# The last down piece of a mixture of experts cut into column halves, gate rows made in the third pair, identity products kept for the first layer only

## What is computed

```
hid = silu(einsum('nd,edf->enf', n, w_gate)) * einsum('nd,edf->enf', n, w_up)
hid = hid * gates.T[:, :, None]
moe = einsum('enf,efd->nd', hid, w_down)
xp = xp + gf_p * moe(prompt rows)
xs = xs + gf_s * moe(sample rows)
```

## Time and profile before

| | |
|---|---|
| median of 3 runs | 1241.68 us (1240.28 to 1242.07) |
| the profiled execution's own time | 1242.56 us |
| its span from first to last instruction | 1240.7 us |
| PE busy | 94% of the span |
| DVE, ACT, POOL busy | 23%, 15%, 5% |
| chain that ended last | PE 74%, DMA 20%, issue 2%, DVE 1% |
| read from HBM | 490.72 MB |

### The profile page before, as it was taken

One profiled execution on the slowest core, in us unless ns is written; L12 is line 12 of the kernel. 1 busy time (PEld: TensorE's weight loads), 2 busy tenths in 40 slices (PEclk: granted clock), 3 DMA queues, 4 the chain that ended last, 5 costly groups with the idle time before them and its releaser, 6 DMA issues.

```text
span 1240.7 us, 13760 instructions
## 1 busy us (share of the span) xinstructions
PE 1170.5 (94%) x5531; PEld 514.7 (41%) x5531; DVE 279.6 (23%) x673; ACT 187.5 (15%) x441; POOL 56.4 (5%) x68
## 2 busy tenths in 40 slices
PE   4999999999998889899999999999999898898998
PEld 2445465443433333334334454743434324343432
DVE  1146533121020101021232354312021010202013
ACT  1225322000000000001022333210000100000010
POOL 0412000000000000000013100000000000000000
PEclk9999999999999999999999999999999999999999
DMA  9999999999999999999998559899999999999996
GB/s 375 389 387 369 415 424 429 423 430 428 429 424 429 430 426 429 430 427 427 421 389 268 196 214 398 359 376 407 426 426 428 427 428 428 429 428 427 430 422 282
DMA packets 60948, 494.18 MB, mean 398 GB/s; under 512 B 5586, under 2 KB 6754, under 8 KB 30052
## 3 DMA queue, kind: packets, MB, share of 16 engines
q1 hardware_dynamic: 57856, 485.88, 94.7%
q0 software_dynamic: 2864, 7.46, 1.8%
q10 hardware_dynamic: 180, 0.17, 0.0%
HBM read 490.72 MB, written 3.16 MB: 398 GB/s over the span
## 4 chain that ended last, share of the span: by engine, by line
PE 74%; DMA 20%; issue 2%; SPq 2%; DVE 1%; ACT 1%; POOL 0%; DVEq 0%; ACTq 0%
PE bank L1195 40%; PE bank L944 9%; DMA ring<-in_w_up 8%; DMA ring<-in_w_gate 5%; DMA ring<-in_w_down 3%; PE bank L1223 3%; PE bank L954 3%; PE bank L1145 3%; DMA ring<-in_w_mod 3%; PE bank L899 3%; PE bank L1156 3%; PE bank L877 2%; PE bank L961 1%; PE bank L1256 1%; PE bank L999 1%
## 5 line engine op out<-in xcount | busy, mean ns | idle before, releaser
L1195 PE MATMUL bank<-ring,hT 128*64 128x512 f32 x2520 | 576.5, 608 | 43.9 <-issue 20.3
L1195 PEld LDWEIGHTS bank<-ring,hT 128*64 128x64 f32 x2520 | 191.0, 140 | 399.8 <-issue 392.2
L944 PE MATMUL bank<-ring,hT 128*128 128x512 f32 x320 | 140.2, 595 | 2.7 <-DMA ring<-in_w_in_ab 2.4
L944 PEld LDWEIGHTS bank<-ring,hT 128*128 128x128 f32 x320 | 59.8, 190 | 78.5 <-issue 75.7
L2014 DVE TENSOR_TENSOR work<-work,bank 128x512 f32<-128x512 f32 x56 | 38.5, 688 | 163.4 <-PE bank L1156 163.2
L2007 DVE TENSOR_TENSOR work<-work,bank 128x512 f32<-128x512 f32 x32 | 22.0, 687 | 221.3 <-PE bank L1195 197.8
L1195 PE MATMUL bank<-work,hT 128*64 128x512 f32 x284 | 69.4, 593 | 0.0
L1145 PE MATMUL bank<-work 128*128 128x128 f32 x512 | 61.4, 278 | 0.3 <-DVE rc L2056 0.3
L1145 PEld LDWEIGHTS bank<-work 128*128 128x128 f32 x512 | 59.8, 195 | 2.0 <-issue 1.6
L1533 ACT ACTIVATE hT<-bank 128x512 f32<-128x512 f32 x32 | 19.0, 595 | 257.3 <-PE bank L1256 257.3
L2066 DVE COPY work<-bank 128x512 f32<-128x512 f32 x14 | 9.7, 692 | 205.5 <-PE bank L1195 205.5
(11 more groups left out here) (223 smaller groups left out, 756.9 us busy)
## 6 DMA issues: line engine op xcount, KB each, us to landing
ring<-in_w_gate SPq DMA_DIRECT2D x56, 2048.0 KB, 17.8
ring<-in_w_up SPq DMA_DIRECT2D x50, 2048.0 KB, 17.2
ring<-in_w_down SPq DMA_DIRECT2D x46, 2048.0 KB, 16.9
ring<-in_w_mod SPq DMA_DIRECT2D x23, 2048.0 KB, 10.9
work<-in_w_up SPq DMA_DIRECT2D x8, 2048.0 KB, 15.2
ring<-in_w_down SPq DMA_DIRECT2D x12, 1024.0 KB, 14.3
ring<-in_w_in_c SPq DMA_DIRECT2D x6, 2048.0 KB, 21.7
ring<-in_w_in_ab SPq DMA_DIRECT2D x4, 2048.0 KB, 21.3
```

The source lines that it names most:

```text
L944: ins = pe.matmul(b[:, 0:n], hT[:, c, t * P:(t + 1) * P], w[:, c, 0:n], start=i == 0, stop=i == DC - 1)
L1195: ins = pe.matmul(bank[banks[j]][64 * e:64 * e + 64, :], lhs[:, 4 * h + c, 64 * e:64 * e + 64], weights(e, c, j), start=(h, c) == (0, 0), ...
```

## The change

Four edits:

- The last piece, row chunk 3 of units 10 and 11, is loaded and multiplied in two: its left 512 columns, then its right 512. `LAST_PIECES` gets a fourth entry, the range of `j`. PE does the scatter of (1, 0) between the two.
- DVE gates in the order (1, 0), (0, 0), (1, 1), (0, 1), so both products of the left bank come first. PE scatters in layer 1 in that order, in layer 0 in the order (1, 0), (1, 1), (0, 0), (0, 1).
- The four matmuls that spread the gate rows, and ACT's four copies, stand in pair 2 in place of the last pair.
- The identity products of t = 1 are made in layer 0 only. In layer 1 all four quarters of `x` are ended by an addition on DVE, and the result is written out in the gating order.

```
-LAST_PIECES = [(6, 0, 2), (6, 2, 4), (8, 0, 2), (8, 2, 4), (10, 0, 2), (10, 2, 3), (10, 3, 4)]
+LAST_PIECES = [(6, 0, 2, range(2)), (6, 2, 4, range(2)), (8, 0, 2, range(2)), (8, 2, 4, range(2)),
+               (10, 0, 2, range(2)), (10, 2, 3, range(2)), (10, 3, 4, range(1)), (10, 3, 4, range(1, 2))]
+GATED_ORDER = [(1, 0), (0, 0), (1, 1), (0, 1)]
+SCATTER_ORDER = {0: [(1, 0), (1, 1), (0, 0), (0, 1)], 1: GATED_ORDER}
...
@@ last_units, SP
-                            cols = slice(D * c0, D * c1)
-                            sp.dma_start(flat[slot][:, cols], src[:, cols]).then_inc(last_ld[l][i], 16)
+                            cols = slice(D * c0 + UC * js[0], D * (c1 - 1) + UC * (js[-1] + 1))
+                            sp.dma_start(flat[slot][:, cols], src[:, cols]).then_inc(last_ld[i], 16)
...
@@ last_product, PE
-                        pe.wait_ge(last_ld[l][i], 32)
-                        for j in range(2):
+                        pe.wait_ge(last_ld[i], 32 * (l + 1))
+                        for j in js:
...
+                        if (k, c1, js[-1]) == (10, 4, 0):
+                            scatter_gated(0)
...
-                def last_scatter():
-
-                    for t in (1, 0):
-                        for h in range(2):
-                            pe.wait_ge(m["yd_gated"], 3 - 2 * t + h)
-                            pe.matmul(last_bank(t, h)[:, :], GT[:, t, :], ydg[t][:, h * UC:(h + 1) * UC],
-                                      start=t == 0, stop=True).then_inc(m["scattered"], 1)
+                def scatter_gated(i):
+
+                    t, h = SCATTER_ORDER[l][i]
+                    pe.wait_ge(m["yd_gated"], 1 + GATED_ORDER.index((t, h)))
+                    pe.matmul(last_bank(t, h)[:, :], GT[:, t, :], ydg[t][:, h * UC:(h + 1) * UC],
+                              start=(l, t) != (0, 1), stop=True).then_inc(m["scattered"], 1)
...
@@ pair, PE
                     if final:
                         scatter(n)
                         gates_transposed(n)
-                        pe.wait_ge(m["y_added"], 4 * n + 4)
-                        expert_gate_rows(1)
-                        expert_gate_rows(0)
                     product(n, 0, (0, 1), hgT, m["hg_ready"])
...
                     product(n, 2, (0, 1), hgT, m["hg_ready"], m["gate_half"])
+                    if isinstance(n, int) and n == 2:
+                        pe.wait_ge(m["y_added"], 4 * n + 4)
+                        expert_gate_rows(1)
+                        expert_gate_rows(0)
...
-                        last_product(n, 8, (6, 7), hidT, None, 0)
+                        last_product(n, 8, (6, 7), hidT, None, None if l else 0)
                         pe.wait_ge(m["ht_ready"], 2 * n + 2)
-                        row_first(n, 1)
+                        if l == 0:
+                            row_first(n, 1)
...
@@ pair, DVE
                     if final:
                         gate_down(1, 0)
+                        gate_down(0, 0)
                         dve.wait_ge(moe_used[l], used(n, 11))
                         gate_down(1, 1)
+                        gate_down(0, 1)
                         return
...
@@ end of layer 1, DVE
-                    gate_down(0, 0)
-                    gate_down(0, 1)
-                    for u in range(2):
-                        row_out(end, u)
-                    for u in range(2):
-                        add_last(end, 0, u)
+                    for t, u in SCATTER_ORDER[1]:
+                        add_last(end, t, u)
```

More of the change, by code:

```diff
@@ L393, in build @@
         moe_ld = [[sem(f"moe_loaded{l}_{i}") for i in range(SLOTS)] for l in range(LAYERS)]
-        last_ld = [[sem(f"last_loaded{l}_{i}") for i in range(len(LAST_PIECES))] for l in range(LAYERS)]
+        last_ld = [sem(f"last_loaded{i}") for i in range(len(LAST_PIECES))]
         ahead_ld = [[sem(f"ahead_loaded{l}_{e}") for e in range(2)] for l in range(LAYERS)]
@@ L634, in last_units @@
                         load_in_turn(k, at[k % 2], n * MOE_UNITS + (k + 1))
-                    for i, (k, c0, c1) in enumerate(LAST_PIECES):
+                    for i, (k, c0, c1, js) in enumerate(LAST_PIECES):
                         w, order = (a["w_up"], "(p h r) -> h p r") if k < 8 else (a["w_down"], "(h p r) -> h p r")
@@ L758, in _ @@
             experts(1)
-            for t, name in ((1, "y_sample"), (0, "y_prompt")):
-                for u in range(2):
-                    cols = slice(u * UC, (u + 1) * UC)
-                    sp.wait_ge(x_ready, 4 * 3 + 2 * (1 - t) + u + 1)
-                    sp.dma_start(a[name][:, cols], x[:, t, cols]).then_inc(out_y, 16)
+            for i, (t, u) in enumerate(SCATTER_ORDER[1]):
+                cols = slice(u * UC, (u + 1) * UC)
+                sp.wait_ge(x_ready, 4 * 3 + i + 1)
+                sp.dma_start(a[("y_prompt", "y_sample")[t]][:, cols], x[:, t, cols]).then_inc(out_y, 16)
             sp.wait_ge(out_y, 64)
@@ L1213, in last_product @@
                     slots = [moe_slot(l, k + e - OUTSIDE) for e in range(2)]
-                    for i, (unit, c0, c1) in enumerate(LAST_PIECES):
+                    for i, (unit, c0, c1, js) in enumerate(LAST_PIECES):
                         if unit != k:
@@ L1295, in pair @@
                         last_product(n, 6, (2, 3), hgT, m["up_half"])
-                        pe.wait_ge(m["gates_ready"], 4)
                     else:
@@ L1300, in pair @@
                         pe.wait_ge(m["y_added"], 4 * n + 4)
+                    if isinstance(n, int) and n == 2:
+                        pe.wait_ge(m["gates_ready"], 4)
                     hidden_transposed(n, 0)
@@ L1328, in experts @@
                 pair(more * PAIRS + (PAIRS - 1), final=True)
-                last_scatter()
+                for i in range(1, 4):
+                    scatter_gated(i)
             pe.wait_ge(ld_first, 16)
@@ L1547, in pair @@
                                    ACT.Copy).then_inc(m["gt_ready"], 1)
-                    if final:
+                    sigmoid(n, 0)
+                    sigmoid(n, 1)
+                    if isinstance(n, int) and n == 2:
                         for i, (t, u) in enumerate(((1, 0), (1, 1), (0, 0), (0, 1))):
@@ L1551, in pair @@
                             act.activation(gbuf[:, 2 * t + u, :], bank[4 + 2 * t + u][:, :], ACT.Copy).then_inc(m["gates_ready"], 1)
-                    sigmoid(n, 0)
-                    sigmoid(n, 1)
                     hidden_transposed(n, 0)
@@ L2039, in add_last @@
                 def add_last(n, t, u):
-                    count, cols = 2 * (1 - t) + u + 1, slice(u * UC, (u + 1) * UC)
+                    count, cols = 1 + SCATTER_ORDER[l].index((t, u)), slice(u * UC, (u + 1) * UC)
                     dve.wait_ge(m["scattered"], 4 * n + count)
```

## The result

| | before | after |
|---|---|---|
| median | 1241.70 us (1240.02 to 1244.80, 8 runs) | 1246.61 us (1244.66 to 1250.48, 8 runs) |
| the profiled execution's time and span | 1242.56, 1240.7 | 1244.66, 1242.9 |

The ratio of after to before is 1.0038, with a 95% interval of 1.0027 to 1.0049: 4.7 us slower. The predicted time was 1246.2 us.

A forecast was written before the change was run, and what follows sets the result against it. The weight stream sets the pace in both mixtures of experts, PE running neck and neck with it in the last pairs. Layer 0's 1.4 + 1.9 and layer 1's 1.3 - 0.1 give +4.5 on 1241.68: 1246.2 us, range 1242.8 to 1248.5.

The forecast's parts named there:

- a lead of 0.3: Last pair, units 4 and 5: PE, ready earlier, starts their product 0.3 us sooner, still held by unit 5's landing.
- the early scatter: Scatter between the last piece's halves delays bank 7's gating: 1.9 us at layer 0's hand-over, 1.3 at layer 1's end.
- Rival D: Layer 0's hand-over: its 1.9 us is partly hidden by other waiting; +1.2 us in all, 1242.9, chance 0.15.
- T: Start of the unit-10 product in a layer's last pair; 1226.59 in layer 1 before the change.
- Rival C: Layer 0's hand-over: the clock falls once more at PE's stops, 1.7 us more; +6.2, 1247.9, chance 0.1.
- The new wait and the early arrival of PE: Last pairs: without the gate rows PE is ready sooner, then waits some 2.7 us for units 4 and 5.
- Rival E: Last pair: PE is the bound and the stream lands early enough to follow; -7.6 us, 1234.1, chance 0.09.
- rival B: Layer 0's last pair: the clock does not fall behind the new wait; +3.0 us in all, 1244.7, chance 0.2.
- So I take a fall here, in both layers: Clock falls behind the wait for units 4 and 5, costing 1.7 us; layer 0's unit-10 product starts 1.4 late.
- The identity products in layer 1: Two products of 1.1 us each leave layer 1's last pair; their 2.2 us absorb the slow clock, unit 10 0.1 early.
- I cost the move at nothing: Gate rows' 3.7 us in pair 2 of each layer cost nothing, covered by PE's waits and the loads' spare time.
- the stream's reserve: Pair 2: the load with least in hand has some 7.6 us of its 17.46 to spare, more than the rows' 3.7.

The follow-up runs named there:

- after_again: The changed kernel, unaltered, run once more: 1246.99 us, ratio 1.0038 against the kernel before.
- rows_back: The changed kernel with the gate rows and their copies back at the head of the last pair: 1244.68 us, ratio 1.0025 against the kernel before.
- rows_at_wait: The changed kernel with the gate rows in the last pair, between its gate and up products: 1245.37 us, ratio 1.0033 against the kernel before.
- scatter_late: The changed kernel with the split kept and all four scatters behind the right half: 1243.29 us, ratio 1.0015 against the kernel before.
- whole_piece: The changed kernel with all four scatters last and the last piece one load and one product again: 1243.28 us, ratio 1.0015 against the kernel before.
- rows_only: The kernel before with only the gate rows moved into pair 2 of both layers: 1243.82 us, ratio 1.0017.
- rows_layer0: The kernel before with the gate rows moved into pair 2 of layer 0 only: 1243.11 us, ratio 1.0006.
- pieces_and_halves: The changed kernel with scatters last, unit 10 in single chunks, layer 0's old gating order, layer 1's gate rows before the last up products: 1241.27 us, ratio 1.0000.
- rows_twice: The kernel before with the gate rows in pair 2 of both layers and each of their matmuls made twice: 1248.44 us, ratio 1.0045.
- rows_layer1: The kernel before with the gate rows moved into pair 2 of layer 1 only: 1243.26 us, ratio 1.0008.
- before_again: The kernel before, unaltered, profiled a second time: 1240.7 us.

## Why the prediction was right, and where it was not

The sum was +4.5, and +4.7 was measured (by the ratio; the medians differ by 4.9). Three of its terms did not hold as they stood. The clock in layer 0 was put at 1.7 us less a lead of 0.3, and comes to some 0.7 less 0.1 on the mean; the move of the gate rows was put at nothing and costs some 0.8; the scatter costs 0.3 more than was said. That the errors nearly cancel is luck: the early scatter was foreseen, the closeness of the sum was not earned.

**The early scatter: right.** It was put at 1.9 us in layer 0 and 1.3 in layer 1. The traces of after, after_again, rows_back and rows_at_wait all have 2.07 and 1.45. Both forecasts are some 0.15 short, because DVE's second pair of gatings began at T + 9.3 and not at T + 9.15. Of layer 0's 2.07, 0.31 stem from the gating order (scatter_late, whole_piece), which the prediction had not told apart. Rival D, that the hand-over is hidden, is out: from PE's first transpose of layer 1 to its first expert product it is 161.3 to 161.5 us in all thirteen traces, whether the transpose comes at T + 11.6 or T + 13.6. Rival C, a fall of the clock in the hand-over, is out too: behind PE's stops the eight transposes take 1.16 us, as before.

**The new wait and the early arrival of PE: right.** 2.87 and 2.86 us, for the predicted 2.7; the relief of 3.7 us bought PE nothing, since unit 5's landing decides. Rival E is out with it. The lead of 0.3 in layer 0 was too large (rival B itself took 0.1): T is 24.95 us behind unit 5's landing in place of 25.02, 0.07.

**"So I take a fall here, in both layers": true of some executions only.** With the rows moved into pair 2 there are seven traces with the new wait of 2.85 to 2.89 us in layer 0, and the clock fell in three (scatter_late, rows_only, rows_layer0); in layer 1, where the waits are of 2.85 to 3.31, it fell in five of seven. (In pieces_and_halves a late landing put the longer wait of layer 0, 3.23, ahead of units 2 and 3; the clock fell there, 8.53, and it cost nothing, for units 4 and 5 were still awaited.) The cost where it fell in layer 0 is 26.64 - 24.95 = 1.7 us as predicted. As a mean the term is 1.7 x 3 / 7 = 0.7 and not 1.7. The profile of after is one without the fall, rival B's. The Trainium skill (TensorE: Matmul & The Clock Gate, Why this matters for your kernels) warns only of idle gaps above a length that all of these waits but the 3.31 stay under. The clock fell behind seven of those thirteen, which speaks against taking its figure for a safe limit.

Where the falls come is not without order: they go with how PE had waited just before. Ahead of the product of units 2 and 3, the one before, PE waited 1.66 to 1.71 us in seven of the fourteen cases, and behind all seven waits for units 4 and 5 the clock fell. It waited 0.90 to 1.10 us in five, and behind none of them it fell. rows_twice has the other two, and they fit less well: 3.16 us before, no fall; 0.88 before, a longer wait of 3.31, and a fall. The pair loops of all thirteen traces lean the same way. Of their waits of 2.5 to 2.6 us with one of 1.6 to 1.8 ahead of the product before, 35 of 38 were followed by a slow product; of those of 2.3 to 2.6 without a wait over 0.3 there, 12 of 42. No run changed the earlier wait by itself, so this is a thing that goes along with the fall, not a shown cause.

**The identity products in layer 1: right, for a reason that rows_only shows.** The prediction let their 2.2 us absorb the slow clock. In rows_only they are still there, and the same fall is paid in full:

```profile
1201.86 8.78 PE L1195 MATMUL bank<-ring,hT 128*64 128x512 f32 x32 [2.86 <-DMA ring<-in_w_up]
...
1228.25 7.09 PE L1223 MATMUL bank<-ring,hT 128*64 128x512 f32 x32
```

T is 26.64 us behind unit 5's landing at 1201.61, with no wait for a load. In after it is 24.97, with 0.51 of waiting. My expectation of rows_layer1, that the fall would be hidden there too, was wrong in its ground, for that kernel keeps the products; its trace happened to have no fall. No run leaves the identity products out alone.

**"I cost the move at nothing": this step failed.** PE's side of it held. In layer 1 after has no wait of PE left where before had the one ahead of 975.37. In layer 0 one of 1.83 us is left, at full clock, and PE then starts the product at 386.96, 193.6 us behind the layer's first one, as in before (388.07). What failed is the stream's reserve. It was worked out on the pair's second load, as 17.46 less two transfers of 4.9, 7.6 us. The first load, that of unit 4, is the tighter one, and the trace of before had it:

```profile
L579 SPq DMA_DIRECT2D ring<-in_w_up x1: 332/332/332, 947.5 to 947.5; - x1
...
DMA to landing us min/median/max: 12.6/12.6/12.6
```

It took 12.6 us there and 11.1 in before_again. Nor could it land 4.9 us behind its issue; on the empty queue of rows_twice it took 7.3. So the reserve was 12.6 - 7.3 = 5.3 us in one execution of the kernel before and 3.8 in the other, and the rows put the issue off by 3.8. With them the load is issued 2.5 to 3.4 us ahead of the landing of the one before it, and some 0.8 us of stream are lost in layer 1 in most executions. This explains that little of the reserve is left, but not the size of the loss: in rows_only the load still took 8.5 us, more than 7.3, and the stream lost 0.9. Why the stream loses time before the reserve is used up, stays open. In layer 0 the same load is issued 6.6 us ahead of that landing in rows_only and 4.7 in rows_twice, nothing is lost, and the step holds.

Put together, with sizes from the traces (the clock as its mean, fall by share of traces), against the ratios:

| kernel | pieces | sum | measured (95%) |
|---|---|---|---|
| after | 2.07 + 1.45 + 0.7 + 0.8 - 0.1 | 4.9 | 4.7 (3.4 to 6.1) |
| rows_at_wait | 2.07 + 1.45 + 0.7 | 4.2 | 4.1 (2.6 to 5.6) |
| rows_back | 2.07 + 1.45 | 3.5 | 3.1 (1.7 to 4.3) |
| scatter_late, whole_piece | 0.31 + 0.7 + 0.8 - 0.1 | 1.7 | 1.9 (0.7 to 3.0) |
| rows_only | 0.7 + 0.8, and 1.7 x 5 / 7 in layer 1 | 2.7 | 2.1 (0.9 to 3.4) |
| rows_layer0 | 0.7 | 0.7 | 0.7 (-0.4 to 1.9) |
| rows_layer1 | 0.8, and 1.7 x 5 / 7 | 2.0 | 1.0 (0.0 to 2.1) |
| rows_twice | 0.7 + 4.1, and 1.7 x 5 / 7 | 6.0 | 5.6 (4.0 to 7.2) |

The sums lie within the intervals, rows_layer1's at the edge of it. The intervals are some 3 us wide, and the sizes are taken from traces of the same kernels, so the table shows that the pieces suffice, not that each is right to a few tenths. What stays open is how often the clock falls: shares of three and five in seven are few cases, and no experiment here steered it.

## What to carry to other kernels

A matmul that waits for another engine, written ahead of matmuls that are ready, delays everything behind it on its engine: starting a tail early pays only if the wait is over when PE gets there. Work taken off an engine that waits for a stream anyway gives nothing, and work added elsewhere is free only while the next load is still issued well ahead. To judge that, take the tightest load and its time on an empty queue (7.3 us here), not what its bytes take (4.9): issued 4.7 us or more ahead of the landing before it, it lost 0.5 us at most, with 2.5 to 3.4 us 0.2 to 1.0, and 0.5 us behind that landing 4.1. And compare stages by their own start: two single spans here differed by 2.1 us where the kernels differ by 4.7.

## What the runs showed of the hardware

- The same kind of wait, 2.85 to 2.91 us ahead of the same product, was followed by a product of 8.78 us or of 7.09 in different traces of kernels that are alike at that place. It was 8.78 in all seven cases in which PE had waited 1.66 to 1.71 us one product earlier, and 7.09 in the five in which that wait was 0.90 to 1.10.
- One load of 2 MB issued on an empty queue (rows_twice, 959.1) took 7.3 us to land, where loads that queue up land 4.9 us apart.
- Within a steady stream of 2 MB loads, which land 4.9 us apart, ten of the thirteen traces have a landing or two in layer 0 that come 6.1 to 6.6 us behind the last one, though issued 8 to 19 us ahead of that one's landing: once in before (301.1), before_again (331.2), after (331.1) and four more, and twice in rows_back, pieces_and_halves and rows_twice, whose unit 5 lands at 602.8 to 604.4 in place of 600.0 to 600.6 in the first three named. They come with and without each of the edits, and at few places: 331 to 336 in six traces, and at 203 to 205 and again at 593 to 595 in the last three. How much of the spread between executions of one kernel they make, no run here shows.
